# Expert matrices of a mixture-of-experts layer loaded 4 MB at a time instead of 2 MB, with TensorE reading gate and up columns at a step of 8

## The reference

```python
def swiglu_expert(xb, wg, bg, wu, bu, wd, bd):
    gate = jnp.minimum(xb @ wg + bg, SWIGLU_LIMIT)
    up = jnp.clip(xb @ wu + bu, -SWIGLU_LIMIT, SWIGLU_LIMIT)
    glu = gate * jax.nn.sigmoid(SWIGLU_ALPHA * gate)
    return ((up + 1.0) * glu) @ wd + bd

def routed_moe(h, wr, br, wg, bg, wu, bu, wd, bd):
    ...
    logits = (hf @ wr + br).astype(jnp.float32)
    top_v, top_i = lax.top_k(logits, TOP_K)
    gates = jax.nn.softmax(top_v, axis=-1)
    ...
    def run_block(args):
        tok, w, e = args
        y = swiglu_expert(hf[tok], wg[e], bg[e], wu[e], bu[e], wd[e], bd[e])
        return y.astype(jnp.float32) * w[:, None]
```

## Time and profile before

| what | value |
|---|---|
| time, median of 3 runs | 1191.02 us (1190.42 to 1191.3) |
| profiled execution: own time | 1193.47 us |
| profiled execution: span from first to last instruction | 1191.1 us |
| PE busy | 1117.3 us, 94% |
| VectorE, ScalarE busy | 251.4 us (21%), 144.9 us (12%) |
| bytes through the DMA engines | 455.90 MB, 383 GB/s over the span |
| mean granted TensorE clock | 0.992 of full speed |

### The profile page before, as it was taken

One profiled execution on the slowest core, in us unless ns is written; L12 is line 12 of the kernel. 1 busy time (PEld: TensorE's weight loads), 2 busy tenths in 40 slices (PEclk: granted clock), 3 DMA queues, 4 the chain that ended last, 5 costly groups with the idle time before them and its releaser, 6 DMA issues.

```text
span 1191.1 us, 12332 instructions
## 1 busy us (share of the span) xinstructions
PE 1117.3 (94%) x5461; PEld 478.3 (40%) x5461; DVE 251.4 (21%) x531; ACT 144.9 (12%) x280; POOL 20.2 (2%) x39
## 2 busy tenths in 40 slices
PE   6899999999999999999999999999999999999885
PEld 1788955443343333333333333333333333333221
DVE  0335760711111112111111111111111111111113
ACT  1222340210010000000000000000000000000001
POOL 0400000000000000000000000000000000000000
PEclk9999999999999999999999999999999999999998
DMA  9996376669999999999999999999999999999992
GB/s 322 334 359 229 115 266 253 276 250 417 430 426 426 429 428 427 429 428 426 429 427 426 429 426 427 429 428 428 429 427 428 428 426 427 429 427 427 429 427 87
DMA packets 55365, 455.90 MB, mean 383 GB/s; under 512 B 4916, under 2 KB 18272, under 8 KB 29584
## 3 DMA queue, kind: packets, MB, share of 16 engines
q1 hardware_dynamic: 52208, 446.72, 90.8%
q0 software_dynamic: 2064, 6.98, 1.8%
q10 hardware_dynamic: 1040, 1.40, 0.5%
HBM read 453.38 MB, written 1.70 MB: 382 GB/s over the span
## 4 chain that ended last, share of the span: by engine, by line
DMA 52%; PE 32%; DVE 2%; issue 0%; ACT 0%; DVEq 0%
DMA ring<-in_w_up 52%; PE bank L1511 21%; PE bank L1383 2%; PE bank L1487 2%; PE bank L1506 1%; PE bank L1522 1%; PE bank L1178 1%; PE bank L1157 0%; PE bank L1185 0%; PE bank L1535 0%; PE bank L1451 0%; PE bank L1551 0%; PE bank L1419 0%; PE bank L1542 0%; DVE xres L984 0%
## 5 line engine op out<-in xcount | busy, mean ns | idle before, releaser
L1511 PE MATMUL bank<-ring,kv_pool 128*64 128x512 f32 x1024 | 229.1, 595 | 16.6 <-DMA ring<-in_w_up 15.2
L1511 PE MATMUL bank<-ring,at_pool 128*64 128x512 f32 x1024 | 228.6, 594 | 15.3 <-DMA ring<-in_w_up 14.4
L1511 PE MATMUL bank<-ring,k_pool 128*64 128x512 f32 x1024 | 231.9, 598 | 9.1 <-DMA ring<-in_w_down 6.9
L1511 PEld LDWEIGHTS bank<-ring,kv_pool 128*64 128x64 f32 x1024 | 70.4, 137 | 170.5 <-issue 125.1
L1511 PEld LDWEIGHTS bank<-ring,at_pool 128*64 128x64 f32 x1024 | 71.1, 137 | 167.7 <-issue 126.0
L1511 PEld LDWEIGHTS bank<-ring,k_pool 128*64 128x64 f32 x1024 | 69.0, 136 | 147.9 <-issue 113.9
L667 ACT COPY k_pool<-bank 128x512 f32<-128x512 f32 x32 | 18.8, 586 | 608.5 <-PE bank L1535 608.5
L1059 DVE COPY cumT<-bank 128x256 f32<-128x256 f32 x32 | 13.6, 424 | 303.3 <-PE bank L1542 303.3
L1065 DVE TENSOR_SCALAR k_pool<-bank 128x512 f32<-128x512 f32 x32 | 22.1, 692 | 255.1 <-PE bank L1511 255.1
L1073 DVE TENSOR_SCALAR k_pool<-bank 128x512 f32<-128x512 f32 x32 | 22.1, 692 | 229.3 <-PE bank L1511 229.3
L1506 PE MATMUL bank<-kv_pool,cst 128*64 128x512 f32 x256 | 68.9, 617 | 0.8 <-ACT at_pool L659 0.8
(11 more groups left out here) (302 smaller groups left out, 572.6 us busy)
## 6 DMA issues: line engine op xcount, KB each, us to landing
ring<-in_w_gate SPq DMA_DIRECT2D x64, 2048.0 KB, 24.2
ring<-in_w_up SPq DMA_DIRECT2D x64, 2048.0 KB, 25.6
ring<-in_w_down SPq DMA_DIRECT2D x64, 2048.0 KB, 24.6
ring<-in_w_mod SPq DMA_DIRECT2D x24, 1024.0 KB, 12.1
ring<-in_w_in SPq DMA_DIRECT2D x13, 1024.0 KB, 14.9
ring<-in_w_out SPq DMA_DIRECT2D x4, 1024.0 KB, 6.9
k_pool<-in_const_masks POOLq DMA_DIRECT2D x1, 1024.0 KB, 8.9
g<-in_b_mod POOLq DMA_DIRECT2D x2, 512.0 KB, 10.9
```

Of the source, the lines that this page charges most:

```text
L1511: ins = mm(bank[CAP * half:CAP * (half + 1), :], lhsT(4 * r + kk), w[:, kk, 512 * half:512 * (half + 1)], start=m == 2 and r == 0 and kk = ...
```

## The change

The 12 slots become three places of 4 MiB (`quad`), one whole matrix in each. A matrix is one load in which partition p holds the eight consecutive rows 8p to 8p+7: a run of 32 KB. Fourteen of the 96 matrices (`HALVED`: numbers 3 to 15 and the last, in the order of loading) come as two loads of four rows a partition (16 KB runs), each with its own semaphore. A whole load waits until both halves of the matrix three before are used; TensorE waits for the whole matrix before its first matmul. The pieces ahead of the mixture use the same slots, shifted by seven (`slot_of`), so that place 0 comes free first.

With eight rows a partition, the two halves of the hidden columns have to be the columns with c in 0 to 3 and in 4 to 7, where column = 8m + c. So TensorE reads the moving operand of gate and up, and of their biases, at a step of eight words (32 bytes), 128 words for each of four c (`half_columns` with `mixed`); down is read in a row as before. In exchange L1076 reads and writes in a row. L989 and L997 reorder in blocks of eight instead of four.

Cut to its core:

```diff
-PAIRS = RING // 2
+QUADS = RING // 4
+HALVED = [j for j in range(3 * NE) if 3 <= j < 16 or j == 3 * NE - 1]
...
+        def slot_of(n):
+            return (n + 7) % RING
+        def matrix_of(m, e):
+            return (at_moe(m, e) - AT_MOE) // 2
+        def quad(j):
+            return ring[:, 4 * (j % QUADS):4 * (j % QUADS) + 4, :].rearrange("p s w -> p (s w)")
+        def piece_slot(j, r):
+            return 4 * (j % QUADS) + (2 * r if j in HALVED else 0)
...
-            def load_rows(view, w, e, r):
-                return sp.dma_start(view.rearrange("p (k n) -> p k n", k=4),
-                                    w[0, bass.ds(e, 1), 512 * r:512 * (r + 1), :].rearrange("a (p k) n -> p (a k) n", p=P))
+            def load_rows(view, w, e, k0, k1):
+                return sp.dma_start(view.rearrange("p (a k n) -> p a k n", a=1, k=KT)[:, :, k0:k1, :],
+                                    w[0, bass.ds(e, 1), :, :].rearrange("a (p k) n -> p a k n", p=P)[:, :, k0:k1, :])
             def load_matrix(m, e):
-                for r in range(2):
-                    if n < AT_MOE + PAIRS:
-                        sp.wait_ge(chunks_used, min(AT_MOE, 32 + 2 * (n - AT_MOE)))
-                    else:
-                        sp.wait_ge(chunks_used, n - PAIRS + 1)
-                    load_rows(pair_rows(n), (w_gate, w_up, w_down)[m], e, r).then_inc(pair_loaded(n), 16)
-                    n += 1
+                j, w = matrix_of(m, e), (w_gate, w_up, w_down)[m]
+                if j < QUADS:
+                    sp.wait_ge(chunks_used, 33 + 4 * j)
+                    load_rows(quad(j), w, e, 0, KT).then_inc(slot_loaded[piece_slot(j, 0)], 16)
+                elif j in HALVED:
+                    for r in range(2):
+                        sp.wait_ge(chunks_used, AT_MOE + 2 * (j - QUADS) + r + 1)
+                        load_rows(quad(j), w, e, 4 * r, 4 * r + 4).then_inc(slot_loaded[piece_slot(j, r)], 16)
+                else:
+                    sp.wait_ge(chunks_used, AT_MOE + 2 * (j - QUADS) + 2)
+                    load_rows(quad(j), w, e, 0, KT).then_inc(slot_loaded[piece_slot(j, 0)], 16)
...
             def pairs(ap):
-                return ap.rearrange("p (r m k) -> p r m k", r=2, k=4)
+                return ap.rearrange("p (m k) -> p m k", k=KT)
...
-                V.scalar_tensor_tensor(ab.rearrange("p (k m) -> p m k", k=4), upb.rearrange("p (m k) -> p m k", k=4), 1.0,
-                                       actb.rearrange("p (m k) -> p m k", k=4), ALU.add, ALU.mult).then_inc(ev("a_ready"), 1)
+                V.scalar_tensor_tensor(ab, upb, 1.0, actb, ALU.add, ALU.mult).then_inc(ev("a_ready"), 1)
...
+            def half_columns(ap, half, mixed):
+                if mixed:
+                    return ap.rearrange("p (m c) -> p c m", c=KT)[:, 4 * half:4 * half + 4, :]
+                return ap[:, 512 * half:512 * (half + 1)].rearrange("p (c m) -> p c m", c=4)
             def product(bank, m, e, lhsT, arrived, pick=None):
+                out = [bank[CAP * half:CAP * (half + 1), :].rearrange("p (c m) -> p c m", c=4) for half in range(2)]
...
-                    w = arrived(m, e, r).rearrange("p (k n) -> p k n", k=4)
-                    for kk in range(4):
+                    w = arrived(m, e, r).rearrange("p (k n) -> p k n", k=KT)
+                    for k in range(4 * r, 4 * r + 4):
                         for half in range(2):
-                            ins = mm(bank[CAP * half:CAP * (half + 1), :], lhsT(4 * r + kk), w[:, kk, 512 * half:512 * (half + 1)],
-                                     start=m == 2 and r == 0 and kk == 0, stop=r == 1 and kk == 3)
+                            ins = mm(out[half], lhsT(k), half_columns(w[:, k, :], half, m < 2),
+                                     start=m == 2 and k == 0, stop=k == KT - 1)
```

More of the change, by code:

```diff
@@ L304, in at_moe, with piece_loads @@
             return AT_MOE + 6 * e + {GATE: 0 if e == 0 else -2, UP: 2, DOWN: 6 if e + 1 < NE else 4}[m]
[L306 to L320, removed]
+        def slot_of(n):
[6 more added lines that the diff above has]
+            return 4 * (j % QUADS) + (2 * r if j in HALVED else 0)
+        def piece_loads(j, r):
+            before = len([n for n in range(AT_MOE) if slot_of(n) == piece_slot(j, r)])
+            mine = [i for i in range(j % QUADS, j + 1, QUADS) if piece_slot(i, 0) == piece_slot(j, r) or piece_slot(i, 1) == piece_slot(j, r)]
+            return 16 * (before + len(mine))
         class Chain:
@@ L361, in load_mod @@
                         src = w_mod[0, 512 * r:512 * (r + 1), m * D + 512 * half:m * D + 512 * (half + 1)]
-                        load(n, ring[:, n % RING, :].rearrange("p (k n) -> p k n", k=4),
+                        load(n, ring[:, slot_of(n), :].rearrange("p (k n) -> p k n", k=4),
                              src.rearrange("(k p) n -> p k n", p=P))
@@ L366, in _ @@
             for k in range(KT):
-                load(n, ring[:, n % RING, :], w_mod[0, P * k:P * (k + 1), 0:2 * D])
+                load(n, ring[:, slot_of(n), :], w_mod[0, P * k:P * (k + 1), 0:2 * D])
                 n += 1
             for b in WIN:
-                load(n, ring[:, n % RING, :].rearrange("p (k n) -> p k n", k=KT),
+                load(n, ring[:, slot_of(n), :].rearrange("p (k n) -> p k n", k=KT),
                      w_in[0, :, 256 * b:256 * (b + 1)].rearrange("(k p) n -> p k n", p=P))
@@ L375, in _ @@
             for r in WOUT:
-                load(n, ring[:, n % RING, :].rearrange("p (k n) -> p k n", k=2),
+                load(n, ring[:, slot_of(n), :].rearrange("p (k n) -> p k n", k=2),
                      w_out[0, 256 * r:256 * (r + 1), :].rearrange("(k p) n -> p k n", p=P))
@@ L412, in _ @@
                         sp.wait_ge(chunks_used, j * 6 + AT_END)
-                        for cidx in range(6):
-                            load_rows(pair_rows(AT_MOE + cidx), (w_gate, w_up, w_down)[cidx // 2], e, cidx % 2).then_inc(ev("over_loaded"), 16)
+                        for m in range(3):
+                            load_rows(quad(m), (w_gate, w_up, w_down)[m], e, 0, KT).then_inc(ev("over_loaded"), 16)
             for t in range(2):
@@ L1175, in mod_sums @@
                     slot_wait(at + r)
-                    w = ring[:, (at + r) % RING, :].rearrange("p (k n) -> p k n", k=4)
+                    w = ring[:, slot_of(at + r), :].rearrange("p (k n) -> p k n", k=4)
                     for j in range(4):
@@ L1219, in project @@
                 slot_wait(n)
-                w = ring[:, n % RING, :].rearrange("p (k n) -> p k n", k=KT)
+                w = ring[:, slot_of(n), :].rearrange("p (k n) -> p k n", k=KT)
                 bank = B[i % 2]
@@ L1378, in project_out @@
                 slot_wait(AT_WOUT + i)
-                w = ring[:, (AT_WOUT + i) % RING, :].rearrange("p (k n) -> p k n", k=2)
+                w = ring[:, slot_of(AT_WOUT + i), :].rearrange("p (k n) -> p k n", k=2)
                 for t in range(2):
@@ L1505, in product @@
                     for half in range(2):
[L1506 removed]
+                        mm(out[half], row, half_columns(mbias, half, True), start=True, stop=False)
                 for r in range(2):
[L1508 to L1509 removed]
+                    w = arrived(m, e, r).rearrange("p (k n) -> p k n", k=KT)
+                    for k in range(4 * r, 4 * r + 4):
                         for half in range(2):
[L1511 to L1512 removed]
+                            ins = mm(out[half], lhsT(k), half_columns(w[:, k, :], half, m < 2),
+                                     start=m == 2 and k == 0, stop=k == KT - 1)
                     ins.then_inc(chunks_used, 1)
```

26 lines of the change are left out of this document (12 added, 14 removed).

## The result

The changed kernel takes 1702.08 us (median of 4 runs, 1699.24 to 1705.92) against 1190.72 us of the kernel before on the same chip: a ratio of 1.4262, with a 95% interval of 1.421 to 1.4314. That is 511 us slower, where 3.6 us faster was forecast.

A forecast was written before the change was run, and what follows sets the result against it. The DMA engines were taken to bound the mixture's end. Fewer packets -6.7 us, the whole load at the end +3.1 us, waits and stepped reads nothing: -3.6 us, a median of 1187.4 us, range 1183 to 1195 us.

The forecast's parts named there:

- What bounds the kernel: Mixture: the DMA engines alone set its end from 248 us on; TensorE has 1.95 us an expert of slack.
- the DMA cost of a packet: Expert loads: 9.4 ns a packet beside its bytes, nine fewer a matrix, 84 ns; 6.7 us saved over 79 matrices.
- the end: Last expert: up 31 as a whole load starts its product only after landing; 3.1 us lost.
- the waits: Mixture, TensorE and DMA waiting on three places: costed at nothing, no wait over 2 us, no fall of the clock.
- the fit: Two stretches with full DMA engines, solved for 9.4 ns a packet and 36.8 us a MB of one engine.
- The first rival: Expert loads: long runs save only 0.7 us, so 2.4 us slower in all, 1193.4 us; chance 0.23.
- the third: Rival: three places are too few, DMA engines stand still in every expert, 1212 us; chance 0.03.
- TensorE's reads at a step of eight: Gate and up products and biases, 15.8 us an expert: they do not become slower; costed at nothing.
- The second rival: Gate and up: each stream holds its own line, every word costs a read; 10.6 us more an expert, 1480 us; chance 0.17.
- The forecast's 0.57: The chance given to the forecast itself, 0.50 of it to faster and 0.07 to a saving that falls short.

The follow-up runs named there:

- row_reads: The changed kernel with gate, up and their biases read in a row again (columns then mismatch down's rows); 1189.73 us against 1191.92 us before, ratio 0.9974.
- one_and_four: The kernel before with a step of 8 in the output projection (one stream) and modulation sums (four streams) instead; 920 and 233 ns an instruction.
- short_runs: `row_reads` with the same 4 MB loads, but two runs of 16 KB a partition instead of one of 32 KB; 29.37 to 29.38 us an expert.
- long_gate_up: The changed kernel reading in a row, gate and up in 32 KB runs, down in two 16 KB runs, up 31 and down 31 halved; 1190.74 us, ratio 1.0.
- all_long: The changed kernel reading in a row, all runs 32 KB, sixteen small products replacing four transposes, up 31 and down 31 halved; 1192.19 us, ratio 1.0006.
- all_long_ends: `all_long` with more loads halved, numbers 3 to 18 and the last six; 1190.61 us, ratio 0.9984.

## Why the prediction was wrong, point by point

**What bounds the kernel, the DMA cost of a packet, the end, the waits.** These held, as `row_reads` shows, but for the longest wait: it was 2.3 us where none over 2 was expected (and the earlier trace rows has 1.4, not 1.3, as the longest before), without a fall of the clock behind it. The saving of an expert was put at 3 x 84 ns = 0.25 us; over the 19 experts up to up 31 it is 29.53 - (1151.50 - 594.81) / 19 = 29.53 - 29.30 = 0.23 us, or 8.5 ns for each of the 27 packets that are gone, where the fit had 9.4. The loss at the end was put at 3.1 us and was 10.27 - 6.93 = 3.3 us. The DMA engines stayed full with three places. The whole came to 2.2 us by the medians, of 3.6 forecast, within the interval; from the first gate product to the start of the last down product the profiled executions take 922.2 us before and 919.3 us in `row_reads`, 2.9 us less. The first rival (the run length buys little) falls with this, and so does the third. The Trainium skill's figure for a packet (DMA: Bandwidth & Descriptors, Why small descriptors are slow), 3 cycles or by estimate 3.5 ns, is under half of what these runs show.

**The step that failed is "TensorE's reads at a step of eight", taken at nothing.** Its argument was: four side-by-side streams bring 4 words in 0.99 ns from four places, so if the read side kept nothing between one stream's word and the next, every word would be a read of its own already. The "if" was the error. A gate or up product went from 6.87 to 14.69 us and a bias from 1.01 to 1.96 us, 17.6 us more of TensorE's time an expert, where 1.69 us were free. The row is as well explained by four streams that each hold a piece of their own, and nothing in the trace before chose between the two. `one_and_four` chooses: each stream takes 1.8 ns for a word at a step, beside others or alone.

**The second rival was right in kind** and had 0.17. It was priced too low, at 1480 us (and 1640 us for a doubling): VectorE's ratio of 1.67 was carried over to TensorE. The time of a word would have come nearer, though two numbers make no rule: VectorE's 1141 ns for 512 words are 2.2 ns a word with the start included, TensorE's price is 1.79 ns. An engine that in a row needs only 0.84 ns a word loses the more by it. With 1.8 ns a word, 512 words in 920 ns, the sum would have been (920 / 430 - 1) x 15.8 = 18 us more an expert, 45.4 us, and 245 + 32 x 45.4 + 17 = 1715 us. The rule of the Trainium skill (Advanced Engine Details and Errata, SBUF Cachelines: lines of 16 bytes, two hits on each for full speed) stood beside that rival. The runs agree with it on TensorE: two words within 16 bytes lose some 5%, one word makes it 2.1 times slower.

**The chances.** The forecast's 0.57 rested on a reading of one row with two explanations, while a row of another engine and a stated rule spoke against it; that was too much. The price of being wrong, 511 us against a gain of 3.6, also meant that the range left out the only case that could matter.

## What to carry to other kernels

Let TensorE's moving operand (f32 here) run in a row, or at most at a step that leaves two words within 16 bytes; reorder on the small side instead, where 512 columns of activations pass once, not on weights that stream through by the megabyte. A full engine has no room for a rearrangement that is "only a pattern": here 3.6 us of transfer were to be had, TensorE had 1.7 us an expert to spare, and the pattern took 17.6. When a transfer engine is the bound, count packets: fewer and longer runs gave 0.23 us of 29.4 here, the same bytes in fewer loads gave none.

## What the runs showed that was not expected

Whole loads make TensorE's waits longer, and after some of them its granted clock fell. In the profiled executions of `row_reads`, `short_runs`, `long_gate_up`, `all_long` and `all_long_ends` a product waited eleven times 2.0 to 2.4 us for its load; five of these products took 8.78 us, the other six 7.09. In `short_runs` a down product (timeline: start us, us, engine line) followed a wait of 2.21 us for its load:

```profile
1115.97 8.78 PE L1527 MATMUL bank<-ring,k_pool 128*64 128x512 f32 x32 [2.21 <-DMA ring<-in_w_down]
```

and took 8.78 us instead of 7.09. The stretches around it, with the granted clock as the third number from the end:

```profile
1100.00:1115.00 15.00, 13.76 (x64) 4.38 (x60) 2.08 (x3) 1.11 (x2) 0.00 (x0) 1.00 1.02 433
1115.00:1118.00 3.00, 2.03 (x6) 0.83 (x8) 0.00 (x0) 0.00 (x0) 0.00 (x0) 0.70 1.00 426
1118.00:1121.00 3.00, 3.00 (x12) 1.13 (x10) 0.00 (x0) 0.00 (x0) 0.00 (x0) 0.73 1.01 431
1121.00:1126.00 5.00, 5.00 (x26) 1.79 (x24) 0.84 (x3) 0.58 (x1) 0.00 (x0) 1.00 1.01 429
```

The clock went from full, 2.4 GHz, to its lower level of 1.2 GHz for part of these 6 us and came back. The five are two in `short_runs` and one each in the last three versions; the three waits of this length in `row_reads` had no such effect, so the length of the wait alone doesn't tell. The prediction expected no wait over 2 us and no fall of the clock; whole loads bring both, though the 1.7 us of the product shown was then hidden by the DMA engines.
